# Single matmuls with their own waits in the first projection groups, and the last tile's stores and square sums block by block, in a hybrid encoder layer

## The chip, the cores and the metric

The kernel runs on the 8 cores of one Trainium2 chip, one stream of the prompt batch and two of the 16 decode streams on each core, with no exchange between cores. The metric is the device time of the slowest core in microseconds (us).

## The reference, cut to what matters

One layer of a streaming encoder (D_MODEL 1024, 8 prompt streams of 8192 frames, 16 sample streams of 16 frames, FFN width 2816):

```python
h = rms_norm(x, p['norm_mix_g'])
u, q, k, v, gl = jnp.split(h @ p['w_in'], SPLITS, axis=-1)
u, new_rnn_conv = causal_dwconv(u, ...)            # width 4
y_rnn, new_h = rglru(u, ...)                       # gates, recurrence
q = rms_norm(q ...); k = rms_norm(k ...)           # per head
y_attn, ... = banded / cached window attention     # ALiBi, sinks
g_rnn, g_attn = jnp.split(jax.nn.sigmoid(gl + p['b_gate']), 2, axis=-1)
mixed = g_rnn * (y_rnn @ p['w_rnn_proj']) + g_attn * (y_attn @ p['w_attn_proj'])
x = x + mixed @ p['w_out']
h2 = rms_norm(x, p['norm_ffn_g'])
a, b = jnp.split(h2 @ p['w_up'], 2, axis=-1)
a, new_ffn_conv = causal_dwconv(a, ...)            # width 3
x = x + (jax.nn.gelu(a) * b) @ p['w_down']
# rms_norm: x * rsqrt(mean(x * x) + 1e-6) * g
```

Outputs are x of both kinds of streams and their new states.

## The kernel before

Activations lie with the 128 features of a block on the partitions and the frames in the free dimension. The prompt stream of a core is cut into NT = 16 tiles of 512 frames; a tile of x is 8 blocks of 128 x 512 in `xt`, which has two buffers. The sample streams (32 columns) go along with tile 0 and share its weights.

A tile has a front half and a back half. The front half is the first norm (`n1`, which writes the 8 blocks of `hTa`), the K, Q, U and V projections with their norms, convolution and recurrence, and the attention (units "K", "Q", "U", "V", "A"). The back half is `mid` (gates and the two branch projections, which write `mq`), `outp` (output projection, residual add, and the second norm, which writes `hTb`), `up` and `down` (the FFN). Class "F" is the front of a tile, class "B" the back of the one before; the two run beside each other, except for the front of tile 0 and the back of tile 15.

A projection group is `mm8`: eight (or six) matmuls of 128x128 weights by 128x512 into one PSUM bank, added as one operation that waits for all its inputs ahead of its first matmul. Its weights are a block in `ring`, which has 11 slots. In tile 0 the blocks come as float32 through GpSimd's queue, which casts them (`ring<-wb`), and SyncE stores each one as bf16 to the scratch `wsc` once it has landed; later tiles load them from there on SyncE's queue (`ring<-wsc`). `load_x` sends four loads of 512 KB on SyncE's queue for each tile.

The order of the instructions is planned ahead. Each operation has a due value `P.v` (smaller is earlier), an engine, and a duration from a small model (`t_pe`, `t_act` and others). `schedule` simulates the engines and takes for each one the ready operation with the smallest due value (ring loads strictly in order); the result is a fixed list for each of the five queues, with semaphore waits between them. The matmul groups of a class share a key, "chainF" or "chainB", so they keep the order in which they were added. The due values of the front of tile 0 start at -1.0 + 0.36 for K0 and grow with the cost of the units (K 3, Q 3, U 7, V 1, A 4, in all 122 for a span of 0.61).

A norm sums the squares of the 8 blocks. `norm_begin(s, nsum)` says how many of them are summed ahead: ScalarE squares each block, GpSimd adds the first nsum squares into one buffer, and TensorE sums that and each of the other squares over the partitions by matmuls with a matrix of ones (L721). With nsum = 1, GpSimd adds nothing and TensorE does one ones matmul per block. The squares have three buffers (`sq`). Before, `outp` uses 6 in every tile, and `n1` uses 1 in tile 0 and 8 in the others. `norm_end` takes Ln and Exp (L728, L730) and scales the blocks on VectorE (L733).

`down` writes back x: block m's residual add (L1081) follows its three groups, and after blocks 3 and 7 one store of 1 MB goes to `yp` on SyncE's queue (L1085). The kernel ends when SyncE has seen all DMA semaphores at their last values.

Of the kernel before, what the change touches and what calls it, by code (L numbers as in the profile page):

```python
# [17 lines left out]
class _DSem:  # L18
    def __init__(self, sem, name):
        self.sem = sem  # L20
        self.name = name
        self.count = 0
        self.last = None
# [56 lines left out]
class Prog:  # L80
    def __init__(self, nc):
        self.nc = nc
        self.ops = []
        self.last_writer = {}
        self.readers = {}
        self.stack = contextlib.ExitStack()
        self.eng_sems = {}
        for e in ("pe", "act", "dve", "pool"):
            self.eng_sems[e] = self.stack.enter_context(nc.semaphore("s_" + e))
        self.dsems = []  # L90
        self.v = 0.0
        self.cls = "B"

    def sbuf(self, name, shape, dtype):
# [321 lines left out]
def t_dve(n):  # L416
    return 0.17 + n / 960.0
# [10 lines left out]
def t_pe(n):  # L428
    return max(n / 2370.0, 0.061)


def build_program(T):
    assert T % 512 == 0
    NT = T // 512
# [5 lines left out]
    def dout(name, shape, dt=F32):  # L440
        return nc.dram_tensor(name, list(shape), dt, kind="ExternalOutput").ap()
# [15 lines left out]
    yp = dout("yp", [NT, 128, 8, 512])  # L457
# [12 lines left out]
    P = Prog(nc)  # L470
    xt = P.sbuf("xt", [128, 2, 8, 512], F32)
# [67 lines left out]
    def sbf(pool, s):  # L539
        return Buf(SMALL[pool.name] if s.id == "s" else pool)  # L540


    d_x = [[P.dsem(f"x{b}{q}") for q in range(4)] for b in range(2)]
    d_y = [[P.dsem(f"y{b}{q}") for q in range(2)] for b in range(2)]
# [11 lines left out]
    def load_x(t):  # L556
        b = t % 2
        for q in range(4):
# [9 lines left out]
          writes=[("hu", s, n) for s in (1, 2) for n in range(8)])  # L568
    P.dma(lambda e: e.dma_start(out=st[:, ST_H + 8:ST_H + 24], in_=sst_d[:, 48:64]), d_c[2],
          writes=[("sh", s, n) for s in (1, 2) for n in range(8)])  # L570
    P.dma(lambda e: e.dma_start(out=st[:, ST_FH + 44:ST_FH + 132], in_=sst_d[:, 64:152]), d_c[3],
          writes=[("fh", s, n) for s in (1, 2) for n in range(NFB)])
# [12 lines left out]
          reads=BT1, writes=BT2, dur=1.3)  # L585
    P.add("dve", lambda e: e.tensor_tensor(out=btf, in0=btf, in1=btf2, op=ALU.max), reads=BT2, writes=BT1, dur=2.3)
    for h in range(8):
# [6 lines left out]
          reads=["prm"], writes=["dv_c"], tset="E")  # L594
    P.add("act", lambda e: e.activation(out=dv[:, DV_CH:DV_CH + 8], in_=dv[:, DV_CH:DV_CH + 8], func=AF.Ln, bias=1.0),
          reads=["dv_c"], writes=["dv_c"], tset="E")
# [11 lines left out]
          reads=["prm"], writes=["dv_esk"], tset="E")  # L608
# [12 lines left out]
    def weight(ti, blk, third=False):  # L621
        buf = Buf(RING)
        n = 768 if third else 1024
        src = w3_d if third else wb_d
        sc = wsc3 if third else wsc
        key = ("w3" if third else "w", blk)
        v0 = P.v
        P.v = v0 - 0.04
        when = 0 if (blk < 50 and not third) else (0, 0, 0, 1, 2)[blk % 5]
        if ti <= when:  # L630
            P.dma(lambda e: e.dma_start(out=buf.t[:, 0:n], in_=src[blk, :, :]), None, reads=XG, writes=[buf], queue="pool", nbytes=128 * n * 4,
                  ringload=True)
            if ti == when:
                ds = d_wst[wst_n[0] % 8]
                wst_n[0] += 1
                P.v = v0
                P.dma(lambda e: e.dma_start(out=sc[blk, :, :], in_=buf.t[:, 0:n]), ds, reads=[buf], writes=[key], nbytes=128 * n * 2)
        else:
            P.dma(lambda e: e.dma_start(out=buf.t[:, 0:n], in_=sc[blk, :, :]), None, reads=[key], writes=[buf], nbytes=128 * n * 2,
                  ringload=True)  # L640
        P.v = v0
        return buf

    def mm8(wbuf, rhs, rkeys, W, nk=8, pbuf=None, start=True, stop=True, k0=0, hold=()):
        if pbuf is None:
            pbuf = Buf(PS)
        fns = []
        for kc in range(nk):
            fns.append(lambda e, kc=kc: e.matmul(pbuf.t[:, 0:W], lhsT=wbuf.t[:, kc * 128:(kc + 1) * 128], rhs=rhs(k0 + kc),  # L649
                                                 start=start and kc == 0, stop=stop and kc == nk - 1))  # L650
        P.add("pe", fns, reads=[wbuf] + list(rkeys), writes=[pbuf, "chain" + P.cls] + list(hold), dur=nk * t_pe(W))
        return pbuf

# [44 lines left out]
    def norm_begin(s, nsum):  # L698
        s.nps = Buf(PS, "G")
        s.nsum = nsum  # L700
        s.nacc = sbf(LT, s)

    def norm_part(s, m):
        W = s.W
        nps, acc = s.nps, s.nacc
        last = s.nsum - 1
        if m == 0 and last > 0:
            P.add("act", lambda e: e.activation(out=acc.t[:, 0:W], in_=s.x(0), func=AF.Square), reads=[s.xk(0)], writes=[acc],
                  dur=t_act(W))
            return  # L710
        sqb = sbf(SQ, s)
        P.add("act", lambda e: e.activation(out=sqb.t[:, 0:W], in_=s.x(m), func=AF.Square), reads=[s.xk(m)], writes=[sqb],  # L712
              dur=t_act(W))
        if m < last:
            P.add("pool", lambda e: e.tensor_tensor(out=acc.t[:, 0:W], in0=acc.t[:, 0:W], in1=sqb.t[:, 0:W], op=ALU.add),  # L715
                  reads=[sqb, acc], writes=[acc], dur=t_pool(W))
            return
        if m == last and last > 0:
            P.add("pool", lambda e: e.tensor_tensor(out=sqb.t[:, 0:W], in0=acc.t[:, 0:W], in1=sqb.t[:, 0:W], op=ALU.add),
                  reads=[sqb, acc], writes=[sqb], dur=t_pool(W))  # L720
        P.add("pe", lambda e: e.matmul(nps.t[:, 0:W], lhsT=onesb[:, :], rhs=sqb.t[:, 0:W], start=(m == last), stop=(m == 7)),  # L721
              reads=[sqb, "onesb"], writes=[nps], dur=t_pe(W))

    def norm_end(s, pg, dst, dkeys):
        W = s.W
        nps = s.nps
        r = sbf(LT, s)
        P.add("act", lambda e: e.activation(out=r.t[:, 0:W], in_=nps.t[:, 0:W], func=AF.Ln, bias=EPS, scale=1.0 / D),  # L728
              reads=[nps], writes=[r], dur=t_act(W, 1), tset="E")
        P.add("act", lambda e: e.activation(out=r.t[:, 0:W], in_=r.t[:, 0:W], func=AF.Exp, scale=-0.5), reads=[r], writes=[r],  # L730
              dur=t_act(W), tset="E")
        for kc in range(8):
            P.add("dve", lambda e, kc=kc: e.scalar_tensor_tensor(out=dst(kc), in0=s.x(kc), scalar=prmc(pg + kc, 1),  # L733
                                                                 in1=r.t[:, 0:W], op0=ALU.mult, op1=ALU.mult),
                  reads=[s.xk(kc), r, "prm"], writes=[dkeys[kc]], dur=t_dve(W))
# [285 lines left out]

    def outp(t, ss, va, vbb):
        for s in ss:
            norm_begin(s, 6)
        for m in range(8):
            P.v = va + (vbb - va) * m / 8.0
            wb = weight(t, B_O + m)
            for s in ss:
                ps = mm8(wb, s.mq, [("mq" + s.id, k) for k in range(8)], s.W)
                P.add("dve", lambda e, s=s, ps=ps, m=m: e.tensor_tensor(out=s.x(m), in0=ps.t[:, 0:s.W], in1=s.x(m), op=ALU.add),  # L1030
                      reads=[ps, s.xk(m)], writes=[s.xk(m)], dur=t_dve(s.W))
                norm_part(s, m)
        P.v = vbb
        for s in ss:
            norm_end(s, P_GF, s.hb, [("hb" + s.id, kc) for kc in range(8)])
# [33 lines left out]
    def down(t, ss, va, vbb):  # L1069
        b = t % 2  # L1070
        for m in range(8):
            P.v = va + (vbb - va) * m / 8.0
            wbs = [weight(t, B_D0 + m), weight(t, B_D1 + m), weight(t, m, third=True)]
            for s in ss:
                W = s.W
                ak = "act" if s.id == "p" else "acts"
                ps = Buf(PS)
                for i, wb in enumerate(wbs):
                    nk = 8 if i < 2 else 6
                    mm8(wb, s.ac, [(ak, 8 * i + k) for k in range(nk)], W, nk=nk, pbuf=ps, start=(i == 0), stop=(i == 2), k0=8 * i)  # L1080
                P.add("dve", lambda e, s=s, ps=ps, m=m: e.tensor_tensor(out=s.x(m), in0=ps.t[:, 0:s.W], in1=s.x(m), op=ALU.add),  # L1081
                      reads=[ps, s.xk(m)], writes=[s.xk(m)], dur=t_dve(W))
            if m % 4 == 3:
                q = m // 4
                P.dma(lambda e, q=q: e.dma_start(out=yp[t, :, 4 * q:4 * q + 4, :], in_=xt[:, b, 4 * q:4 * q + 4, :]), d_y[b][q],  # L1085
                      reads=[("x", b, 4 * q + i) for i in range(4)], queue="sp", nbytes=1048576)
        for s in ss:
            if s.id == "s":
                P.dma(lambda e: e.dma_start(out=ys[:, :, :], in_=xss[:, :, :]), d_fin, reads=[("xs", m) for m in range(8)])
# [194 lines left out]
```

How the kernel before makes its waits and increments, by code:

```python
        def emit(name, e, tail=False):  # L354
            for op in streams.get(name, []):
                for sem, val in op.waits:
                    e.wait_ge(sem, val)
                ins = None
                for fn in op.fns:
                    ins = fn(e)
                if op.is_dma:
                    ins.then_inc(op.dsem.sem, 16)
                elif op.needs_sig:
                    ins.then_inc(eng_sems[name], 1)
            if tail:
                for sem, val in finals:
                    e.wait_ge(sem, val)
```

## Time and profile before

| | |
|---|---|
| median of 3 runs | 3942.33 us (4266.44, 3921.73 and 3942.33) |
| profiled execution | 3919.15 us, span of its slowest core 3917.5 us |
| spans of the eight cores | 3899.3 to 3917.5 us |
| TensorE (PE) busy | 3779.3 us, 96% of the span |
| VectorE (DVE), ScalarE (ACT), GpSimd (POOL) busy | 2591.8, 2808.4, 464.6 us |
| mean granted clock of TensorE, slowest core | 0.991 |

The profile is of one execution, on its slowest core, core 6. A line of it names the line of the kernel (L649), the engine, the operation, and the tiles it writes and reads (out<-in). "PE" is the matmul part of TensorE, "PEld" its weight loads, "SPq" the queue of SyncE. Idle time stands with what ended it.

### The profile page before, as it was taken

Reading aid. Unit: us, or ns where it says so; the run is one execution under the profiler, and the core shown is the slowest. Engines: PE = TensorE matmul, PEld = TensorE weight load, DVE = VectorE, ACT = ScalarE, POOL = GpSimd, SP = SyncE. Lnnn points to the kernel's source line nnn. Section 1 sums busy time; section 2 is a strip of 40 time slices with the busy share of each in tenths; the row PEclk is TensorE's granted clock in tenths of the full one; section 3 lists DMA queues with packets and bytes.
Section 4 is the critical chain, followed back from the end, with each engine's and each line's share of the span. In section 5 each row is a group of like instructions: output and inputs, shape, how many; then the busy total and the mean of one; then the engine's idle time right before and its main releaser. Section 6 shows DMA issues by size and latency. Waiting matters only on the chain.

```text
span 3917.5 us, 65207 instructions; the slowest of 8 cores (3899.3 to 3917.5 us)
## 1 busy us (share of the span) xinstructions
PE 3779.3 (96%) x18209; PEld 1746.1 (45%) x18576; DVE 2591.8 (66%) x4718; ACT 2808.4 (72%) x4636; POOL 464.6 (12%) x984
## 2 busy tenths in 40 slices
PE   5789999999999999999999999999999999999989
PEld 2344444444444444444444444444444444444434
DVE  6667476675757757576675757767576675757634
ACT  6778586776868768686776868768686776868641
POOL 2222111111010010101001010010111001011000
PEclk9899999999999999999999999999999999999999
DMA  9598767566464554646446464554645455464544
GB/s 187 117 191 175 199 157 195 149 159 193 134 186 138 157 163 138 190 135 183 141 144 182 134 186 138 160 163 139 188 138 181 140 148 175 139 186 140 159 133 140
DMA packets 325198, 626.69 MB, mean 160 GB/s; under 512 B 36784, under 2 KB 55376, under 8 KB 320720
## 3 DMA queue, kind: packets, MB, share of 16 engines
q1 hardware_dynamic: 299936, 577.87, 49.4%
q0 software_dynamic: 24912, 44.64, 8.1%
q8 instruction: 161, 2.64, 0.3%
q14 instruction: 189, 1.55, 0.1%
HBM read 600.36 MB, written 67.09 MB: 170 GB/s over the span
## 4 chain that ended last, share of the span: by engine, by line
PE 85%; DVE 5%; DMA 4%; ACT 3%; issue 3%; POOL 0%; SPq 0%; DVEq 0%; ACTq 0%; POOLq 0%
PE ps L649 78%; DVE hTb L733 2%; DMA xt<-xp 2%; PE ps L907 1%; PE ps L828 1%; PE ps L963 1%; PE ps L937 1%; DMA yp<-xt 1%; DMA ring<-wb 1%; PE ps L958 1%; DMA ring<-wsc 1%; PE ps L873 1%; DVE fset L754 0%; ACT L970 0%; PE ps L721 0%
## 5 line engine op out<-in xcount | busy, mean ns | idle before, releaser
L649 PE MATMUL ps<-hTb,ring 128*128 128x512 bf16 x5517 | 1259.8, 379 | 33.5 <-DVE hTb L733 18.2
L649 PE MATMUL ps<-hTa,ring 128*128 128x512 bf16 x4246 | 1003.3, 383 | 20.1 <-DMA ring<-wsc 5.8
L649 PEld LDWEIGHTS ps<-hTb,ring 128*128 128x128 bf16 x5632 | 547.0, 98 | 693.6 <-issue 45.3
L649 PEld LDWEIGHTS ps<-hTa,ring 128*128 128x128 bf16 x4352 | 426.1, 99 | 529.6 <-issue 37.2
L649 PE MATMUL ps<-actb,ring 128*128 128x512 bf16 x2762 | 629.0, 380 | 3.4 <-issue 0.2
L754 DVE SCALAR_TENSOR_TENSOR tt<-ps,prm_s,tt 128x511 f32<-128x511 f32 x704 | 522.0, 745 | 50.3 <-POOL tt L750 23.2
L649 PEld LDWEIGHTS ps<-actb,ring 128*128 128x128 bf16 x2816 | 275.8, 98 | 332.5 <-issue 3.2
L747 ACT ACTIVATE tt<-ps,prm_s 128x512 f32<-128x512 f32 x352 | 271.1, 771 | 133.0 <-PE ps L649 131.4
L996 ACT ACTIVATE tt<-ps,dv 128x512 f32<-128x512 f32 x256 | 173.8, 679 | 265.2 <-PE ps L649 256.7
L1065 DVE TENSOR_TENSOR actb<-ps,tt 128x512 bf16<-128x512 f32 x352 | 238.6, 684 | 145.2 <-PE ps L649 144.7
L754 DVE SCALAR_TENSOR_TENSOR fset<-ps,prm_s,fset 128x511 f32<-128x511 f32 x372 | 276.6, 744 | 21.5 <-POOL fset L750 11.6
L1008 DVE TENSOR_TENSOR mq<-ps,tt 128x512 bf16<-128x512 f32 x128 | 88.4, 691 | 274.0 <-PE ps L649 118.1
L830 ACT ACTIVATE fset<-ps,dv 128x512 f32<-128x512 f32 x248 | 157.0, 684 | 150.6 <-PE ps L828 150.1
L715 POOL TENSOR_TENSOR lt<-lt,sq 128x512 f32<-128x512 f32 x154 | 180.0, 1169 | 624.3 <-ACT sq L712 617.4
L649 PE MATMUL ps<-yr,ring 128*128 128x512 bf16 x1003 | 233.9, 380 | 1.3
L649 PE MATMUL ps<-ya,ring 128*128 128x512 bf16 x1003 | 232.9, 379 | 1.1
L649 PE MATMUL ps<-mq,ring 128*128 128x512 bf16 x1003 | 225.1, 379 | 3.2 <-DVE mq L1018 1.6
L1081 DVE TENSOR_TENSOR xt<-ps,xt 128x512 f32<-128x512 f32 x128 | 87.9, 687 | 211.6 <-PE ps L649 211.5
L1061 ACT ACTIVATE tt<-tt 128x512 f32<-128x512 f32 x352 | 205.6, 622 | 18.3 <-DVE tt L754 13.3
L750 POOL TENSOR_TENSOR tt<-tt,hcf 128x2 f32<-128x2 f32 x330 | 76.2, 231 | 1186.9 <-ACT tt L747 1186.5
L1015 DVE TENSOR_TENSOR mb<-ps,tt 128x512 bf16<-128x512 f32 x128 | 88.3, 690 | 176.8 <-ACT tt L1000 92.4
L943 ACT ACTIVATE pT<-lt 128x512 bf16<-128x512 f32 x254 | 155.9, 623 | 41.8 <-DVE lt L940 38.3
(193 smaller groups left out, 4781.6 us busy)
## 6 DMA issues: line engine op xcount, KB each, us to landing
ring<-wsc SPq DMA_DIRECT2D x1731, 256.0 KB, 2.7
ring<-wb POOLq DMA_DIRECT2D x157, 256.0 KB, 6.1
xt<-xp SPq DMA_DIRECT2D x64, 512.0 KB, 6.8
yp<-xt SPq DMA_DIRECT2D x32, 1024.0 KB, 5.3
wsc<-ring SPq DMA_DIRECT2D x118, 256.0 KB, 5.5
ring<-wsc SPq DMA_DIRECT2D x117, 192.0 KB, 2.4
ring<-w POOLq DMA_DIRECT2D x11, 192.0 KB, 5.7
wsc<-ring SPq DMA_DIRECT2D x8, 192.0 KB, 5.7
```

The source lines that it names most:

```text
L649: fns.append(lambda e, kc=kc: e.matmul(pbuf.t[:, 0:W], lhsT=wbuf.t[:, kc * 128:(kc + 1) * 128], rhs=rhs(k0 + kc), start=start and kc == 0, ...
L715: P.add("pool", lambda e: e.tensor_tensor(out=acc.t[:, 0:W], in0=acc.t[:, 0:W], in1=sqb.t[:, 0:W], op=ALU.add), reads=[sqb, acc], writes=[ ...
L747: P.add("act", lambda e: e.activation(out=acc()[:, 0:W], in_=ps.t[:, 0:W], func=AF.Identity, bias=bcol, scale=wcol(ntap - 1)), reads=[ps] ...
L754: P.add("dve", lambda e, k=k: e.scalar_tensor_tensor(out=segv(acc()[:, 0:W], s)[:, :, k:L], in0=segv(ps.t[:, 0:W], s)[:, :, 0:L - k], scal ...
L830: P.add("act", lambda e, pg=pg, col=col, dvc=dvc: e.activation(out=fs.t[0][:, col, 0:W], in_=pg.t[:, 0:W], func=AF.Exp, scale=-1.0, bias=d ...
L943: P.add("act", lambda e, sb=sb, pt=pt, nk=nk: e.activation(out=pt.t[0:nk, 0:N], in_=sb.t[0:nk, 0:N], func=AF.Exp), reads=[sb], writes=[pt] ...
L996: P.add("act", lambda e, g=g, ps=ps, half=half, m=m, W=W: e.activation(out=g.t[:, 0:W], in_=ps.t[:, 0:W], func=AF.Exp, bias=dv[:, DV_NBG + ...
L1008: P.add("dve", lambda e, g=g, ps=ps, s=s, m=m, W=W: e.tensor_tensor(out=s.mq(m), in0=ps.t[:, 0:W], in1=g.t[:, 0:W], op=ALU.mult), reads=[g ...
L1015: P.add("dve", lambda e, g=g, ps=ps, mb=mb, W=W: e.tensor_tensor(out=mb.t[:, 0:W], in0=ps.t[:, 0:W], in1=g.t[:, 0:W], op=ALU.mult), reads= ...
L1061: P.add("act", lambda e, g=g, W=W: e.activation(out=g.t[:, 0:W], in_=g.t[:, 0:W], func=AF.Gelu), reads=[g], writes=[g], dur=t_act(W), tset ...
L1065: P.add("dve", lambda e, g=g, ps=ps, s=s, i=i, W=W: e.tensor_tensor(out=s.ac(i), in0=ps.t[:, 0:W], in1=g.t[:, 0:W], op=ALU.mult), reads=[g ...
L1081: P.add("dve", lambda e, s=s, ps=ps, m=m: e.tensor_tensor(out=s.x(m), in0=ps.t[:, 0:s.W], in1=s.x(m), op=ALU.add), reads=[ps, s.xk(m)], wr ...
```

## The change

A new value `vsplit` = -0.61 stands in the program. In `mm8`, where a group has a key for each of its inputs and its due value is below `vsplit`, each of its matmuls is added as an operation of its own, which waits for its own input block only. In the last tile, `norm_begin` in `outp` is called with 1 in place of 6, and `down` stores each block of x on its own (256 KB), on the eight semaphores of the x loads.

```diff
+        self.vsplit = -0.61
...
         for kc in range(nk):
             fns.append(lambda e, kc=kc: e.matmul(pbuf.t[:, 0:W], lhsT=wbuf.t[:, kc * 128:(kc + 1) * 128], rhs=rhs(k0 + kc),
                                                  start=start and kc == 0, stop=stop and kc == nk - 1))
+        if len(rkeys) == nk and P.v < P.vsplit:
+            for kc in range(nk):
+                P.add("pe", fns[kc], reads=[wbuf, rkeys[kc]], writes=[pbuf, "chain" + P.cls] + (list(hold) if kc == 0 else []), dur=t_pe(W))
+            return pbuf
         P.add("pe", fns, reads=[wbuf] + list(rkeys), writes=[pbuf, "chain" + P.cls] + list(hold), dur=nk * t_pe(W))
         return pbuf
...
     def outp(t, ss, va, vbb):
         for s in ss:
-            norm_begin(s, 6)
+            norm_begin(s, 6 if t < NT - 1 else 1)
...
-            if m % 4 == 3:
-                q = m // 4
-                P.dma(lambda e, q=q: e.dma_start(out=yp[t, :, 4 * q:4 * q + 4, :], in_=xt[:, b, 4 * q:4 * q + 4, :]), d_y[b][q],
-                      reads=[("x", b, 4 * q + i) for i in range(4)], queue="sp", nbytes=1048576)
+            st_ = 4 if t < NT - 1 else 1
+            if m % st_ == st_ - 1:
+                m0 = m + 1 - st_
+                P.dma(lambda e, m0=m0: e.dma_start(out=yp[t, :, m0:m0 + st_, :], in_=xt[:, b, m0:m0 + st_, :]),
+                      d_y[b][m0 // 4] if t < NT - 1 else d_x[m % 2][m // 2],
+                      reads=[("x", b, m0 + i) for i in range(st_)], queue="sp", nbytes=262144 * st_)
```

## Rows read from the trace of the kernel before

**Rows 1.** The page: its head, busy time, and the span in 40 slices.
```profile
span 3917.5 us, 65207 instructions; the slowest of 8 cores (3899.3 to 3917.5 us)
...
PE 3779.3 (96%) x18209; PEld 1746.1 (45%) x18576; DVE 2591.8 (66%) x4718; ACT 2808.4 (72%) x4636; POOL 464.6 (12%) x984
...
PE   5789999999999999999999999999999999999989
```

**Rows 2.** Timeline, VectorE and TensorE, 16 to 30 us.
```profile
16.25 5.39 DVE L733 SCALAR_TENSOR_TENSOR hTa<-xt,prm_s,lt 128x512 bf16<-128x512 f32 x8 [1.83 <-ACT lt L730]
...
21.55 1.38 DVE L733 SCALAR_TENSOR_TENSOR hTas<-xss,prm_s,lt_s 128x32 bf16<-128x32 f32 x8
...
21.89 3.57 PE L649 MATMUL ps<-hTa,ring 128*128 128x512 bf16 x8 [4.64 <-DVE hTas L733]
...
25.51 2.99 PE L649 MATMUL ps<-hTa,ring 128*128 128x512 bf16 x8
...
29.55 1.89 PE L649 MATMUL ps<-hTa,ring 128*128 128x512 bf16 x8 [0.62 <-ACT sq L871]
```

**Rows 3.** Timeline and waits of SyncE's queue, and GpSimd's issues, to 30 us.
```profile
18.37 0.33 SPq L637 DMA_DIRECT2D wsc<-ring  x1
...
28.73 0.32 SPq L637 DMA_DIRECT2D wsc<-ring  x1
...
SPq L357 <- DMA ring<-wb: 22.3, 4, 10.0
...
22.90 2.13 POOL L631 DMA_DIRECT2D ring<-wb  x4
...
26.28 0.54 POOL L631 DMA_DIRECT2D ring<-wb  x1 [1.24 <-PE ps L649]
```

**Rows 4.** Windows: busy PE, PEld, DVE, ACT, POOL; granted clock, DMA share, GB/s.
```profile
20.00:30.00 10.00, 7.49 (x37) 3.23 (x39) 2.94 (x11) 2.09 (x6) 6.28 (x13) 1.00 1.06 186
60.00:160.00 100.00, 62.43 (x319) 25.76 (x323) 75.62 (x212) 74.55 (x200) 12.44 (x22) 0.78 0.51 113
80.00:120.00 40.00, 26.38 (x112) 10.07 (x113) 29.67 (x83) 27.40 (x76) 2.65 (x5) 0.67 0.43 103
```

**Rows 5.** Chain of work, 20 to 66 us: start, us, what.
```profile
26.28 24.85 DMA ring<-wb
...
51.62 12.81 DMA xt<-xp
```

**Rows 6.** Timeline of ScalarE, 25 to 66 us.
```profile
25.55 0.60 ACT L871 ACTIVATE sq<-ps 128x512 bf16<-128x512 f32 x1 [7.70 <-PE ps L649]
...
64.79 0.63 ACT L708 ACTIVATE lt<-xt 128x512 f32<-128x512 f32 x1 [4.43 <-DMA xt<-xp]
```

**Rows 7.** Timeline, output projection and norm of tile 15.
```profile
3771.76 13.97 PE L649 MATMUL ps<-mq,ring 128*128 128x512 bf16 x63 [1.58 <-DVE mq L1018]
...
3784.34 1.16 POOL L719 TENSOR_TENSOR sq<-lt,sq 128x512 bf16<-128x512 f32 x1 [0.85 <-ACT sq L712]
...
3785.84 0.69 DVE L1030 TENSOR_TENSOR xt<-ps,xt 128x512 f32<-128x512 f32 x1 [1.03 <-PE ps L649]
3786.68 0.63 ACT L712 ACTIVATE sq<-xt 128x512 bf16<-128x512 f32 x1 [1.09 <-DVE xt L1030]
...
3794.99 2.72 PE L649 MATMUL ps<-hTb,ring 128*128 128x512 bf16 x6 [7.16 <-DVE hTb L733]
```

**Rows 8.** Timeline of the end, from 3894 us.
```profile
3894.13 0.32 SPq L639 DMA_DIRECT2D ring<-wsc  x1
...
...
3912.19 0.34 SPq L1085 DMA_DIRECT2D yp<-xt  x1
```

**Rows 9.** DMA, 3906 to 3918 (40 slices); last, ring loads, 3860 to 3918.
```profile
DMA  0000000000000000000000099999989400000000
...
yp<-xt SPq DMA_DIRECT2D x1, 1024.0 KB, 4.1
...
DMA to landing us min/median/max: 2.3/2.7/4.3
```

## Prediction

> **What bounds the kernel now.** I read the page first: TensorE is busy for 3779.3 of 3917.5 us [rows 1], so only 138 us of the span are not matmul, and a change that removes no large group of matmuls can move the end only by what it does to those gaps. The slices of the page show where they are: the digits of PE are below 9 in the first three slices (294 us) and in the last but one [rows 1]. So two places matter, the start of tile 0 and the end of tile 15, and the change touches just these. Between them every slice reads 9.
>
> At the start, the timeline shows that the first projection group (K0, eight matmuls) begins at 21.89 us, 4.64 us after TensorE's last work, and that what it waited for is VectorE: the eight hTa blocks take 5.39 us from 16.25 on [rows 2]. It looks like a plain 5 us to be had. But the queue of SyncE tells of the weights. Each ring slot, once its weight block has landed, is stored to the scratch by SyncE, in order; of these stores K1's goes out at 18.37, K0's before it, and U0's not before 28.73, after a wait for ring<-wb of 10.0 us [rows 3]. So U0's weights land at about 28.7, and its group starts at 29.55 [rows 2]: the third group has 0.85 us of room and no more. The DMA share of the stretch is 1.06 [rows 4], so the loads don't come sooner for being awaited sooner. Further on the chain of work runs over DMA altogether: the load issued at 26.28 lands 24.85 us later, the load of the next tile's x goes out behind it at 51.62 and takes 12.81 us [rows 5], and ScalarE, whose order is fixed, sits idle for 4.43 us until 64.79 for that very x [rows 6]. From there to about 160 us, tile 0 alone, with nothing of another tile's back half beside it, is bound by short chains of TensorE, ScalarE and VectorE: TensorE is busy for 62.43 us of 100 at a granted clock of 0.78 [rows 4].
>
> At the end, the output projection of tile 15 runs without a gap (63 recorded matmuls in 13.97 us), then comes the norm: residual add, square, ones matmul, Ln, Exp, eight hTb blocks of the same kind and shape as hTa's, and the next group 7.16 us after TensorE's last work [rows 7]. After the last matmul there are a residual add (0.69 us for one of this shape [rows 7]), a store of 1 MB issued at 3912.19 [rows 8], and its landing 4.1 us after its issue [rows 9].
>
> **The change, part by part.**
>
> *Which groups are split.* The due value of K0 is -0.64, of K1 -0.625, of U0 -0.61, and -0.61 is not below -0.61 (in floating point neither). So four groups, K0 and K1 for the prompt and for the 32-column sample stream, become 32 single operations. The back halves start at 0. Nothing is added to TensorE's work.
>
> *Start of tile 0.* K0's last matmul can't start before the eighth hTa block is done at 21.64; with the 0.25 us that lie between that and the 21.89 of before [rows 2], it ends at about 22.3. The chain key keeps the order K0, K0 sample, K1. The sample blocks hTas are done at 21.55 + 1.38 = 22.93, so K1 starts at about 23.2 in place of 25.51 [rows 2]: 2.3 us earlier. Its eight matmuls cost 0.427 us each (3.57 for eight, the lower of the two clock levels, 1.2 GHz) to 0.216, so K1 ends 1.9 to 3.4 us sooner. Then U0 is next, and its weights come at 28.7: at most 29.55 - 28.73 = 0.8 us of this gets past it. The norm steps of K0 and K1 on ScalarE (idle for 7.70 us ahead of the square at 25.55 [rows 6]) move into idle time. On the other path, the ring load at 26.28 waited for K0's slot; GpSimd, busy with issues to 25.03 [rows 3], can send it the 1.24 us of its wait earlier, into queues that are full (1.06), so the landing at 51.1 and the x after it gain between 0 and 1.24 us. I take -0.4 us, near the lower end, because both full queues [rows 4, 5] and the late U0 weights speak against more. The bounds are 0 and -3.4.
>
> *Waits in a row.* The split puts up to eight waits on TensorE's queue where one stood. Behind them stand only the same groups, which could not have run earlier; V0 and V1, whose weights were there, stay behind U0. A wait costs no more than the 0.25 us above, and only the last of each group lies on the path: already counted.
>
> *Squares of tile 15 on TensorE.* Removed: five GpSimd adds (four at 1.16 us each and the one at 3784.34, which ends at 3785.5) and with them the wait for them. None is on the path: the add of block 5 is over at 3785.50, before the residual add of block 7 starts at 3785.84, and the chain goes on from that one over its square at 3786.68 [rows 7]. Added: five ones matmuls, for blocks 0 to 4. Before, three ran, for 5 and 6 after the last projection matmul, in the shade of block 7's add, and for 7. A square is ready some 1.8 us after its group ends (0.05 + 0.69 + 0.10 + 0.63 and the signals), a group lasts 1.73, so by the list's rule (lowest due value among what is ready) the matmuls for 0 to 4, and the one for 5 too, once the groups have grown longer by them, come ahead of the last projection group. That is six of 0.216 us (16 matmuls in 3.62 less the pipeline's end; 0.216 by the spacing) = 1.3 us on a stretch where TensorE has no gap; five would be 1.1. Squares hold one of three buffers until a matmul has read it, instead of an add: no new wait, at one square per 1.9 us. So +1.3 us, bounds 0 and +1.5. The 7.16 us wait for hTb is as before, since nothing of tile 15 is split, and with it the matmuls at the lower clock behind it (six in 2.72 us [rows 7]).
>
> *Stores per block.* Eight of 256 KB in place of two of 1 MB, on their own semaphores, last used by loads long landed. Six more issues of 0.34 us on SyncE's queue, each of which waits for its residual add, with ring loads behind. The last ring load goes out at 3894.13 for a group that starts after 3906 [rows 8], so the loads run eleven slots ahead; a store holds the queue for a block's add and its own issue, 0.69 + 0.34, about 1 us against over 12: hidden, at nothing. If that cover were gone it would cost up to eight times 1 us. The last store now carries a quarter. In the row of the last store the DMA engines are at work in some eight and a half slices of 0.3 us, 2.5 us for 1.05 MB [rows 9]; a quarter of that is 0.6, so 1.9 us less. By the nearest rows of that size, ring loads of 192 to 256 KB at 2.3 to 4.3 us from issue to landing, median 2.7 [rows 9], it would be 1.8 to -0.2, with a median of 1.4. I take -1.7, between the two and nearer to the first, which is of this very store; bounds -1.9 and 0.2.
>
> The Trainium skill (DMA: Bandwidth & Descriptors, section Bandwidth) speaks against small transfers: batch to 1 MiB or more for three quarters of peak. Its fit for a GpSimd-issued transfer (section Anatomy of one DMA) is a fixed 2.0 us plus size over 436 GB/s; taken over to this store as an estimate, that gives 4.4 and 2.6 us, so 1.8 us less where the sum has 1.7. The row's 4.1 us is near the 4.4. The rule is about throughput, and here only the last landing is on the path.
>
> **Sum.** -0.4 + 1.3 - 1.7 = -0.8 us on a profiled execution of 3919.15 us: 3918.3. The two timed runs that are of use for it lie 2.6 and 23.2 us above the profiled one (3921.73 and 3942.33; the third is 8% off and says nothing of the kernel). I set the lower of the two shifts on top: **3921 us**, no change. The median of 3942.33 is that of the shown three and is itself one of those two runs.
>
> **The rivals.**
>
> *The whole start is passed on.* If the U0 weights are not what holds U0 (nearer loads can land sooner on other cores), the 3.0 us and more of K1's end go straight through. For it: from 66 to 160 us nothing but latency bounds, so a shift would stay. Against it: rows 3 and the 4.43 us wait for x. Price -3.4 in place of -0.4: 3918 us.
>
> *The upper clock comes earlier.* Before, TensorE stood idle for 4.64 us ahead of K0 and ran K0 at 0.427 us a matmul. After, it has a matmul every 0.67 us from 16.9 on, and K1 may run wholly at 0.216 (2.4 GHz). K1 then ends 3.4 us sooner and not 1.9, and if those 1.5 us reach the end beside what the sum has, it is 3919.5 us. U0's late weights are against it. The Trainium skill (TensorE: Matmul & The Clock Gate, section The HAM clock gate) says that the idle state is the throttled one and that activity lifts it, which is that mechanism.
>
> *Slower: the list is planned anew.* The order of all engines comes from a list planner with its own durations. In its plan K0 and K1 end 2 to 3 us earlier, so from 22 us on close calls on five queues fall otherwise, and this may cost more than the edits bring. The place is ScalarE's wait for the next tile's x [rows 6]: the squares stand in its queue at a planned place. If they come two or three operations earlier, x lands no sooner, and ScalarE's idle 4.43 us grow by as much work, up to double; and from there on nothing hides it until 160 us. With more gaps, the clock falls as in the stretch of 80 to 120 us (granted 0.67, TensorE busy for 26.38 of 40 us [rows 4]); 20 us more of such a stretch, with 13.2 us of matmul at 0.67 in place of the 0.78 of the whole, give 2.2. Together 4.4 + 2.2 = 6.6: 3928 us. It decides once the squares are planned before the work that now fills ScalarE up to 60.36. For it: the eight cores, with one program, already differ by 18.2 us in span (3899.3 to 3917.5 [rows 1]). Against it: it can as well go the other way.
>
> *It doesn't do what it says.* If SyncE's or VectorE's blocks come too late for the split, only the end is changed: -0.4: 3921 us, not to be told apart.
>
> **How the numbers follow.** No change as summed 0.55; whole start passed on 0.13 and earlier clock 0.07, both to be read as up to 3 us faster; planned anew and slower 0.20; without effect 0.05. No case comes near 2% (78 us), about what a measurement of this kernel can tell from no change. So the range is set less by the cases (3918 to 3928, and 3915 to 3930 with the bounds of the terms) than by how the runs scatter: 18 us between cores, 20.6 between the two runs. I take 3904 to 3944. Faster by over 2%: 0.01; slower: 0.01, for a planner gone astray; within: 0.98.
>
> **What would show it.** Right: the first K0 matmul near 17 us and K1 ending by 25 to 27, with U0 still at 28.7 to 29.5; x of tile 1 landing at 64 to 65. The ones matmuls between the groups of the last output projection, and hTb's first block 1.3 us further behind the projection's first matmul than the 17.6 us of now. The last store landing 2.3 to 2.7 us after issue. Wrong: U0 starting with K1's end, or TensorE's busy time and clock in 60 to 160 us off by over 4 us; a store in the last tile with a ring load behind it that a group waits for.

## The result, and the profile after

The changed kernel takes 3950.99 us (median of 18 runs, 3941.66 to 4677.77) against 3937.27 us of the kernel before beside it (18 runs, 3921.73 to 4539.34). The ratio is 1.0046, 95% interval 1.0026 to 1.0066: about 18 us slower (0.46% of 3.94 ms), small beside 2% but clear of no change, and above the range of the prediction. A few executions of both kernels are disturbed by some per cent; the ratios leave these out.

The page of the changed kernel, head, busy time, slices:

```profile
span 3957.5 us, 65593 instructions; the slowest of 8 cores (3922.1 to 3957.5 us)
...
PE 3817.1 (96%) x18581; PEld 1750.7 (44%) x18581; DVE 2589.5 (65%) x4718; ACT 2803.5 (71%) x4634; POOL 457.6 (12%) x979
...
PE   5788999999999999999999999999999999999989
```

Against [rows 1] the eight spans have moved as a whole: mean 3935.6 us in place of 3911.3, so 24.3 us. That is one execution of each, and the profiled one of before (3919.15 us) was quicker than all of the 18 timed ones, so the 24.3 us say more than the ratio's 18. (The busy sum of TensorE can't be compared: the trace of before lacks some matmul records, x18209 beside x18581.) One digit has changed, the fourth slice, 9 to 8: about 297 to 396 us. The page after is that of core 3, though, and the page before that of core 6; on core 6 no digit has changed. The start and the end, which the prediction read, show in the timeline of TensorE on core 6 what was expected of them, or more:

```profile
17.05 0.59 PE L650 MATMUL ps<-hTa,ring 128*128 128x512 bf16 x1 [0.37 <-DVE hTa L738]
17.43 0.23 PE L726 MATMUL ps<-sq_s,onesb 128*128 128x32 bf16 x1
17.61 4.56 PE L650 MATMUL ps<-hTa,ring 128*128 128x512 bf16 x7
...
23.48 2.72 PE L650 MATMUL ps<-hTa,ring 128*128 128x512 bf16 x6
...
26.07 1.01 PE L650 MATMUL ps<-hTa,ring 128*128 128x512 bf16 x2
...
28.09 1.67 PE L650 MATMUL ps<-hTa,ring 128*128 128x512 bf16 x7 [0.80 <-ACT sq_s L876]
```

K0's first matmul is at 17.05 in place of 21.89, K1 begins at 23.48 in place of 25.51, U0 at 28.09 in place of 29.55 [rows 2]. At the other end, the norm of tile 15 and the DMA slices of 3906 to 3926 us on core 6:

```profile
3780.39 5.34 PE L650 MATMUL ps<-mq,ring 128*128 128x512 bf16 x24 [1.58 <-DVE mq L1023]
...
3804.86 1.44 PE L650 MATMUL ps<-hTb,ring 128*128 128x512 bf16 x3 [7.16 <-DVE hTb L738]
```
```profile
DMA  6400049000000009400000004900000000940000
...
yp<-xt SPq DMA_DIRECT2D x4, 256.0 KB, 2.0
```

Projection to hTb takes 24.47 us in place of 23.23 [rows 7], and the last store lands 2.0 us after its issue in place of 4.1 [rows 9]. These two nearly cancel. So the loss is in neither place that the diff touches.

To find it I compared the starts of the same groups, core by core, in the two timelines. Tile 0's first output-projection group (`ps<-mq,ring`) starts at 219.8 us before (mean of eight cores, 214 to 222) and at 235.8 after (232 to 239). Tile 1's starts at 486.9 before and 511.5 after, tile 3's at 960.0 and 984.0. So 16 us are lost by the start of tile 0's output projection, 8.6 more by tile 1's, and nothing after that. (By how much such starts scatter among kernels with the same list is said with the table below.) TensorE on core 6 at the first of these places, before and then after:

```profile
217.79 1.89 PE L649 MATMUL ps<-ya,ring 128*128 128x512 bf16 x8
219.51 0.35 PE L649 MATMUL ps<-yas,ring 128*128 128x32 bf16 x8
219.72 1.91 PE L907 MATMUL ps<-wvs,hTa 128*128 128x256 bf16 x16
222.29 1.67 PE L649 MATMUL ps<-mq,ring 128*128 128x512 bf16 x7 [0.67 <-DVE mb_s L1015]
...
240.46 1.89 PE L649 MATMUL ps<-hTa,ring 128*128 128x512 bf16 x8
```
```profile
217.74 1.89 PE L650 MATMUL ps<-ya,ring 128*128 128x512 bf16 x8
219.47 0.35 PE L650 MATMUL ps<-yas,ring 128*128 128x32 bf16 x8
221.96 0.83 PE L650 MATMUL ps<-hTa,ring 128*128 128x512 bf16 x2 [2.14 <-DMA ring<-wsc]
...
225.14 2.13 PE L912 MATMUL ps<-wvs,hTa 128*128 128x256 bf16 x16
231.94 3.14 PE L650 MATMUL ps<-hTa,ring 128*128 128x512 bf16 x8 [4.66 <-DMA ring<-wsc]
234.87 2.36 PE L650 MATMUL ps<-mq,ring 128*128 128x512 bf16 x8
```

The last `ya` groups of tile 0 start within 0.05 us of each other in the two kernels: the 1.5 us won at U0 are gone by then. After is even one group behind, because U2 of tile 1 ran ahead of this `ya` group before and runs behind it after, at 221.96, where its weights are late by 2.14 us. Then the order differs once more. Before, the output projection runs at once, and the K0 group of tile 1 (`hTa`) comes behind it, at 240.46. After, this K0 group stands ahead of the output projection. Its weights are not there: TensorE waits 4.66 us, with the eight `mq` groups behind it. The chain of work there (start, us, what):

```profile
196.64 11.07 DMA ring<-wb
...
207.84 11.03 DMA wsc<-ring
...
218.94 12.76 DMA ring<-wsc
...
231.94 5.30 PE ps L650 x16
```

The 256 KB block for K0 is a load from the scratch on SyncE's queue. Three transfers hang on each other here by the ring slot that they share: a casting load of GpSimd fills the slot (11.07 us), SyncE stores the block to the scratch (11.03 us), and only when this store has landed, and TensorE has used the block, may the load for K0 overwrite the slot. It goes out at 218.94 and lands 12.76 us later. The queue ahead of it is held up too: its stores wait for casting loads to land (SyncE's waits from 205 to 240 us: 21.8 us in 9 waits for `ring<-wb`). The load isn't later than before, where K0's load goes out at 222.76, behind six stores; it is the group that now wants it at 227 us and not at 240. TensorE's waits for `ring<-wsc` from 100 to 520 us on core 6, before, then after:

```profile
PE ps L649 <- DMA ring<-wsc: 5.8, 3, 2.9
```
```profile
PE ps L650 <- DMA ring<-wsc: 15.0, 6, 4.7
```

(us in total, times, longest.) Over the eight cores these sums are 2.5 to 5.8 us before and 15.0 to 24.2 after. The idle time is not all of the loss. With the output projection late, what follows from it is late, and less is there to run: from 205 to 245 us TensorE is busy for 32.80 us in place of 37.36, at a clock of 0.91 in place of 1.00 (same columns as [rows 4]):

```profile
205.00:245.00 40.00, 37.36 (x293) 20.01 (x298) 23.72 (x54) 28.18 (x66) 16.26 (x25) 1.00 0.97 201
```
```profile
205.00:245.00 40.00, 32.80 (x228) 16.94 (x231) 20.64 (x47) 22.89 (x55) 7.13 (x14) 0.91 0.87 180
```

### The profile page after: what moved, and what is told of

It reads as the page before. It is cut to its first block, busy times and chain, and to the rows that moved or that the text cites. A ratio compares the mean times of both kernels' runs of the same rounds, so it can differ in the third digit from the quotient of the medians.

```text
span 3957.5 us, 65593 instructions; the slowest of 8 cores (3922.1 to 3957.5 us)
## 1 busy us (share of the span) xinstructions
PE 3817.1 (96%) x18581; PEld 1750.7 (44%) x18581; DVE 2589.5 (65%) x4718; ACT 2803.5 (71%) x4634; POOL 457.6 (12%) x979
## 4 chain that ended last, share of the span: by engine, by line
PE 83%; DMA 7%; DVE 4%; ACT 2%; issue 2%; POOL 1%; SPq 0%; DVEq 0%; ACTq 0%; POOLq 0%
PE ps L650 77%; DMA xt<-xp 2%; DVE hTb L738 2%; DMA yp<-xt 2%; DMA ring<-wsc 1%; DMA ring<-wb 1%; PE ps L912 1%; PE ps L968 1%; PE ps L833 1%; PE ps L942 1%; PE ps L963 1%; PE ps L878 1%; ACT L975 0%; DVE fset L759 0%; POOL lt L720 0%
## 5 line engine op out<-in xcount | busy, mean ns | idle before, releaser
L650 PE MATMUL ps<-hTb,ring 128*128 128x512 bf16 x5632 | 1272.6, 380 | 23.3 <-DVE hTb L738 18.2
L650 PE MATMUL ps<-hTa,ring 128*128 128x512 bf16 x4352 | 1018.6, 384 | 26.5 <-DMA ring<-wsc 24.2
L650 PEld LDWEIGHTS ps<-actb,ring 128*128 128x128 bf16 x2816 | 275.7, 98 | 332.5 <-issue 3.4
```

## The experiments

The theory after the result: the list was planned anew, because in the planner's simulation K0 and K1 end earlier, and a close call then fell the wrong way, tile 1's K0 group ahead of tile 0's output projection. The main rival: the added waits themselves cost time. In the table "mq0" and "mq1" are the starts of the first output-projection group of tile 0 and tile 1, "span" the mean of the eight spans, each in us and a mean over the cores in the profiled execution. "All" is the mean of the eight spans over all executions that enter the ratio, with their number. Lines of helpers shift by a few from kernel to kernel; the tiles' names say which group is meant.

| kernel | ratio [95%] | mq0 | mq1 | span | all |
|---|---|---|---|---|---|
| before | | 219.8 | 486.9 | 3911.3 | 3912.7 to 3913.7 (12, 23, 18) |
| after | 1.0046 [1.0026, 1.0066] | 235.8 | 511.5 | 3935.6 | 3937.2 (13) |
| split only | 1.0052 [1.0037, 1.0068] | 233.0 | 503.5 | 3932.6 | 3929.4 (6) |
| end only | 0.9997 [0.9975, 1.0019] | 219.2 | 489.8 | 3912.6 | 3913.1 (10) |
| waits only | 1.0006 [0.9993, 1.0018] | 220.2 | 485.9 | 3906.4 | 3912.8 (10) |
| plan only | 1.0062 [1.0046, 1.0077] | 233.6 | 509.2 | 3935.9 | 3931.2 (4) |
| K0 held | 1.0010 [0.9978, 1.0042] | 222.4 | 489.9 | 3913.7 | 3916.9 (8) |
| K0 first | 1.0018 [0.9988, 1.0048] | 231.8 | 503.1 | 3925.1 | 3923.1 (4) |
| loads swapped | 1.0041 [1.0013, 1.0068] | 231.3 | 500.2 | 3923.1 | 3928.3 (12) |
| K0 split | 1.0045 [1.0018, 1.0072] | 231.5 | 506.0 | 3932.0 | 3927.8 (9) |
| best | 0.9977 [0.9949, 1.0005] | 220.3 | 491.2 | 3911.6 | 3908.6 (6) |
| plan late | 1.0005 [0.9985, 1.0025] | 228.0 | 499.5 | 3919.0 | 3916.1 (10) |
| plan slow | 1.0007 [0.9990, 1.0024] | 219.4 | 503.3 | 3921.5 | 3923.0 (8) |

Before ran beside the other kernels in three sets, so it has three values in the last column. Beside after, its spans weren't kept; by its slowest core it was some 8 us longer there than in the later sets, so 3937.2 can't be set against them. A standard error of 0.5 to 2 us belongs to each value of the last column (from the scatter of the executions).

End only, waits only and best have the list of before up to tile 14, split only and plan only that of after: the planner does not see the waits or the last tile's edits there. So the scatter of one profiled execution can be read off. With before's list mq0 is 219.2 to 220.3 and mq1 comes 265.7 to 270.9 us later; with after's list mq0 is 233.0 to 235.8 and mq1 270.5 to 275.7 us later. By the means of the two groups the new list costs 14.3 us at mq0 and 5.3 us more at mq1.

**Split only.** The split of the groups, with the last tile as before.

```diff
-            norm_begin(s, 6 if t < NT - 1 else 1)
+            norm_begin(s, 6)
...
-            st_ = 4 if t < NT - 1 else 1
+            st_ = 4
...
-                      d_y[b][m0 // 4] if t < NT - 1 else d_x[m % 2][m // 2],
+                      d_y[b][m0 // 4],
```

> Only the split of the four K groups; the end of the last tile is as before. The theory (the split changes the planned order on all queues, and in tile 0 and 1 loads of tile 1's weights then stand behind stores that wait for cast loads): the whole loss is here, 3946 to 3956 us, ratio 1.003 to 1.007, TensorE idle for weights between 215 and 235 us. The rival that the edits at the end cost it: the time of before, ratio 0.998 to 1.001.

Measured 1.0052, the whole of the loss; by the last column 15.7 us, less than the 24.3 us between the two profiled executions.

**End only.** No group is split; ones matmuls and stores of tile 15 as in the change.

```diff
-        self.vsplit = -0.61
+        self.vsplit = -9.99
```

> Only the edits at the end of the last tile (ones matmuls for all squares, eight stores); no split. By the sum: +1.3 us in the output projection and -1.7 us at the last landing, so the time of before within 2 us (ratio 0.999 to 1.001), and both terms to be read in the trace. The rival that the end costs the time: ratio 1.003 to 1.007.

Measured 0.9997 [0.9975, 1.0019]: the edit of the last tile neither costs nor brings anything that can be told.

**Waits only.** The group stays one planned operation, so each queue keeps the order of before; only at emission does each matmul wait for its own block.

```diff
+        op = P.add("pe", fns, reads=[wbuf] + list(rkeys), writes=[pbuf, "chain" + P.cls] + list(hold), dur=nk * t_pe(W))
+        if len(rkeys) == nk and P.v < P.vsplit:
+            op.late = {P.last_writer[rkeys[kc]]: kc for kc in range(nk)}
...
-                for fn in op.fns:
+                for i_, fn in enumerate(op.fns):
+                    for sem, val in wt.get(i_, ()):
+                        e.wait_ge(sem, val)
                     ins = fn(e)
```

> The planned order of before on every queue, but each matmul of K0 and K1 (both streams) waits for its own block only; the end as before. If the wait itself costs or brings something it is seen here: by the sum -0.4 us, so ratio 0.998 to 1.001, with K0's first matmul near 17 us and U0's group still at 28.7 to 29.5. The theory of the planned order says the same: no loss. A rival in which the waits block TensorE says 1.003 or more.

**Plan only.** The reverse: single operations in the planner, so its order is that of split only, but after planning the first matmul of a group waits for all blocks (`lw` holds their writers).

```diff
+                o_ = P.add("pe", fns[kc], reads=[wbuf, rkeys[kc]], writes=[pbuf, "chain" + P.cls] + (list(hold) if kc == 0 else []), dur=t_pe(W))
+                if kc == 0:
+                    o_.grp = lw
...
         for op in order:
+            if op.grp:
+                op.deps = set(op.deps) | set(op.grp)
```

> The planned order of split_only on every queue, but the first matmul of each K group waits for all eight blocks, as before the change; the end as before. The theory of the planned order: the whole loss stays, ratio 1.003 to 1.007, TensorE idle between 215 and 235 us. The rival of the waits: the time of before.

These two decide the main question. Waits only: K0 starts at 16.59 and U0 at 27.25, two us ahead of before, as early as in the changed kernel, and the ratio is 1.0006 [0.9993, 1.0018]. Plan only: K0 starts at 20.90, so the early start is taken away, and the ratio is 1.0062 [1.0046, 1.0077], with the output projection behind the K0 group of tile 1 again (core 6):

```profile
220.50 1.91 PE L921 MATMUL ps<-wvs,hTa 128*128 128x256 bf16 x16
229.92 3.57 PE L656 MATMUL ps<-hTa,ring 128*128 128x512 bf16 x8 [7.51 <-DMA ring<-wsc]
233.28 2.65 PE L656 MATMUL ps<-mq,ring 128*128 128x512 bf16 x8
```

The waits cost nothing; the order of the list carries the loss.

**K0 held.** The split, and one rule for the planner: tile 1's K0 group (`k0[0]`) only after the seventh output-projection block of tile 0 (`mq[6]`).

```diff
     def finish(self, pen=0.1, bw=300000.0):
+        k0[0].deps.add(mq[6][0].idx)
         self.schedule(pen, bw)
```

> The plan of split_only, with one more rule for the planner: the K0 group of tile 1 comes after the first matmul group of block 6 of tile 0's output projection, as it stands in the order of before. The theory (K0 of tile 1, whose weights come late, stands in front of output projection groups that are ready): the first output projection group starts at 220 to 226 us again in place of 231 to 236, and the ratio falls from 1.0052 to 1.000 to 1.003. The rival that the loss comes from the order of tile 0's front or of SyncE's queue in itself: 1.004 to 1.007, as split_only.

**K0 first.** No split at all, and the opposite rule.

```diff
+        mq[0][0].deps.add(k0[0].idx)
         self.schedule(pen, bw)
```

> The order of before (no split, end as before), with one rule put into the planner: the first output projection group of tile 0 comes after the K0 group of tile 1. The theory: this alone brings the loss, first output projection group at 230 to 236 us, ratio 1.002 to 1.006. The rival (the position of this group is of no matter): 0.998 to 1.001.

Core 6 with K0 held, then with K0 first:

```profile
220.16 1.91 PE L917 MATMUL ps<-wvs,hTa 128*128 128x256 bf16 x16
222.29 1.89 PE L655 MATMUL ps<-mq,ring 128*128 128x512 bf16 x8 [0.23 <-DVE mq L1028]
```
```profile
219.95 1.91 PE L917 MATMUL ps<-wvs,hTa 128*128 128x256 bf16 x16
230.72 3.26 PE L655 MATMUL ps<-hTa,ring 128*128 128x512 bf16 x8 [8.87 <-DMA ring<-wsc]
233.81 1.89 PE L655 MATMUL ps<-mq,ring 128*128 128x512 bf16 x8
```

Held, the output projection starts where it did before, the waits for `ring<-wsc` on core 6 are 2.2 us, and the mean span is within 2.4 us of before's. Put first in a kernel that is otherwise before's, the group brings a wait of 8.87 us, 12 of the 16 us at mq0 and 13.8 of the 24.3 us of the mean span. The timed ratios, which go by the slowest core, say less: 1.0010 and 1.0018, with intervals that touch both 1 and the changed kernel's; by them alone, K0 held could still be 0.4% slower, and K0 first no slower at all. The last column tells them apart: K0 first is 10.4 us longer than before (3923.1 against 3912.7), K0 held 4.2 us, where split only is 15.7. K0 held keeps U2 of tile 1 behind the last `ya` group, as after has it, which may be its 2.6 us at mq0.

**Loads swapped.** The split; on SyncE's queue each load from the scratch of tile 1 that stands right behind a 256 KB store goes one place ahead of it.

```diff
+        for o in [o for o in sp if o.ringload and o.v < 0.5]:
+            i = sp.index(o)
+            if not sp[i - 1].ringload and sp[i - 1].nbytes == 262144:
+                sp[i - 1], sp[i] = sp[i], sp[i - 1]
```

> split_only, with every load of tile 1's weights on SyncE's queue, where it stands right behind a store to the scratch and is due before 0.5, put one place ahead of that store (six to seven such swaps); nothing else of the order is changed. If the loads are late because they stand behind stores that wait for cast loads, each is issued 2 to 5 us sooner and TensorE's waits for ring from the scratch fall from 14 to 20 us to 6 to 14: ratio 1.001 to 1.004. If they are late by the full DMA queues only: as split_only, 1.004 to 1.007.

Measured 1.0041 [1.0013, 1.0068], mq0 231.3, 1.7 us sooner than in split only; the last column has 3928.3 in place of 3929.4. TensorE's waits for `ring<-wsc` are 8.2 to 17.3 us, on six cores within the 6 to 14 expected. The chain of core 6 shows why one place on the queue brings so little:

```profile
192.06 10.24 DMA ring<-wb
...
202.42 12.51 DMA wsc<-ring
...
215.00 8.99 DMA ring<-wsc
```

The moved load goes out at the moment at which the store of the block that stood in its ring slot has landed; so it does on seven of the eight cores, where these stores take 10.97 to 14.01 us. What holds the load is its slot as much as its place on the queue.

**K0 split.** Only K0 of tile 0 is split (bound -0.63). The planner gives here too an order with K0 of tile 1 ahead of the output projection (K1 of tile 1 comes right behind the first group of it, not ahead as the expectation has it), so this is a test on a kernel that the theory was not made from.

```diff
-        self.vsplit = -0.61
+        self.vsplit = -0.63
```

> Only the groups of K0 are split (threshold -0.63 in place of -0.61), the end as before. The planned order that this gives has not only K0 of tile 1 but K1 of tile 1 too ahead of the output projection. The theory: a smaller edit at the start, and the loss is there all the same, first output projection group at 234 to 242 us, ratio 1.003 to 1.008. The rival that the loss grows with the number of split groups: half of that of split_only, 1.002 to 1.003.

Measured 1.0045 [1.0018, 1.0072], mq0 231.5, below the 234 to 242 us expected. Half of the split costs as much as the whole: what counts is the order that comes out. The mean of mq0 is mixed, though: on cores 4 and 5 TensorE is busy without a gap from 180 to 220 us at a granted clock of 0.81 in place of 1.00, core 5 has no wait for weights there at all, and core 4's 238.0 is of the clock. The six other cores give 230.5.

**Best.** The order of before with the waits by block as in waits only, also in the first hTb group of tile 15, and that tile's stores per block; its squares stay on GpSimd.

```diff
+        if len(rkeys) == nk and (P.v < P.vsplit or P.v == P.vlast):
+            op.late = {P.last_writer[rkeys[kc]]: kc for kc in range(nk)}
...
+            st_ = 4 if t < NT - 1 else 1
```

> The planned order of before; the four K groups and the first group on the last tile's hTb wait block by block where they stand; the last tile's stores by block; the square sums as before (GpSimd, six). By the terms: -0.4 for the start, -3 for hTb (its eight matmuls paced by VectorE's 0.67 us in place of 3.4 us behind it), -1.7 for the last store: -5 us, ratio 0.9975 to 1.000.

TensorE of core 6, the first hTb blocks:

```profile
3791.64 0.38 PE L659 MATMUL ps<-hTb,ring 128*128 128x512 bf16 x1 [2.42 <-DVE hTb L745]
3792.30 0.38 PE L659 MATMUL ps<-hTb,ring 128*128 128x512 bf16 x1 [0.29 <-DVE hTb L745]
```

The wait is 2.42 us in place of 7.16 [rows 7], and from the output projection's first matmul to the issue of the last store it is 138.2 us in place of 140.4. The ratio is 0.9977 [0.9949, 1.0005]: it leans to faster, and can't be told from no change.

**Plan late, plan slow.** On top of best, the planner is told that the transfers of this stretch take longer, in the hope that it then puts no group ahead of its weights: all casting loads and the scratch loads of tile 1 land 8 us later, or the bandwidth is three quarters up to tile 1.

```diff
-                op.end = dma_free + 1.9
+                op.end = dma_free + 1.9 + (8.0 if op.eng == "pool" or (op.ringload and op.v < 1.0) else 0.0)
```
```diff
-                dma_free = begin + op.nbytes / bw
+                dma_free = begin + op.nbytes / (bw if op.v > 1.0 else 0.75 * bw)
```

> The kernel best, but the planner is told that cast loads, and loads of tile 1's weights, land 8 us later than it has believed. The order that this gives has the loads of tile 1 one to three stores further ahead on SyncE's queue and no K group ahead of the output projection. The theory (the loss comes from a plan that believes weights to be there too early): TensorE's waits for weights from the scratch fall below the 3 to 8 us of best, first output projection group at 216 to 222 us, ratio 0.994 to 0.999. The rival that any new plan is as good as another: anything from 0.998 to 1.006.

> The kernel best, but the planner reckons with three quarters of its DMA rate for all that is due before tile 1's back half, in place of a later landing. As plan_late by the theory: 0.994 to 0.999; by the rival 0.998 to 1.006. If the two differ, it tells whether it is the landing or the rate that the planner has wrong.

The waits for `ring<-wsc` did go: none from 100 to 520 us in the first, at most 1.5 us on a core in the second, where best has 3.4 to 8.0. The gain didn't come: 1.0005 and 1.0007, against 0.994 to 0.999 expected, and by the last column plan slow is 10 us longer than before, though its slowest core isn't. In plan late mq0 is 228.0 where 216 to 222 was expected; cores 2 and 3 have 239.8 and 240.3 there, at a granted clock of 0.81 from 180 to 220 us, and the six others 223.9 in the mean. mq1 is at 499.5 and 503.3, later than best's 491.2. In plan slow the time went into the stretch of 300 to 400 us; core 4, best, then plan slow (PE busy and count, clock, DMA share, GB/s):

```profile
300.00:400.00 100.00, 95.22 (x709) 1.00 0.92 174
```
```profile
300.00:400.00 100.00, 88.16 (x609) 0.97 0.78 155
```

The new orders have new waits elsewhere. I didn't follow these to a single operation.

## Why the prediction was wrong

**What failed.** The prediction gave "no change as summed" 0.55 and "planned anew and slower" 0.20. The second is what happened, for the reason that it names (the list's close calls fall otherwise, because K0 and K1 end earlier in its plan). So the sum failed by the term that it doesn't have: it leaves the new plan at nothing, where the runs show some 16 us. It was left out because the rival was priced at the wrong place, and this is the failed step: "The place is ScalarE's wait for the next tile's x". That wait did grow, from 4.43 us until 64.79 [rows 6] to this on core 6:

```profile
63.87 0.63 ACT L713 ACTIVATE lt<-xt 128x512 f32<-128x512 f32 x1 [6.92 <-DMA xt<-xp]
```

But x landed 0.9 us sooner, TensorE's busy time from 60 to 160 us is 60.73 us in place of 62.43 [rows 4], within the bound of 4 us that the prediction set, and at 217.8 us the two kernels are level. The place is 150 us further on, where tile 0's back half and tile 1's front first meet, and the engine is TensorE: its order is fixed too, and a group with late weights holds eight groups that are ready. The size followed from the place: 6.6 us were priced; some 18 were timed, and 15.7 by the last column of the table for the split alone.

**Why it could have been seen.** The reading stopped at 160 us, since every slice from the fourth on says 9. The window of 205 to 245 us of before, shown above, was there to be read: DMA share 0.97, and SyncE waits in it, in total, times, longest:

```profile
SPq L357 <- DMA ring<-wb: 27.6, 10, 6.9
```
A load from the scratch issued there stands behind stores that stand behind casting loads. TensorE had at that place two classes of ready work to choose from, of which one hung on this queue. The prediction's ground against the rival, "it can as well go the other way", is true of a plan with correct durations. The planner's are too short here: in its own simulation the three transfers of the chain above (casting load, store, load for K0) take 6.6, 6.9 and 6.3 us, against 11.07, 11.03 and 12.76 measured. That such a plan leans to one side, to put groups ahead of their weights, is argued and not shown: plan late and plan slow, with longer durations, lost the waits and not the time.

**Why the range failed.** It took 3904 to 3944 from the scatter of cores and runs, and its cases went up to 3928. At the size that the runs then showed (16 us at mq0, 24 in the profiled spans), the rival would have stood at 3937 to 3945 on the same base. Of the 30 us by which the forecast missed (3951 against 3921) some 18 are the change, by the ratio. The other 12 are the base: 3921 was the lower of two runs, and beside the change only 1 of the 18 executions of before came as low as 3922.

**Terms that held.** *Start:* K0 "near 17 us" was 17.05, K1 "at about 23.2" was 23.48, and it ended at 27.1 as foreseen at the later side. U0 came 1.5 us sooner (2.3 in waits only) where 0.8 was the most allowed. Its weights still held it, but they were not as fixed as taken: SyncE's store of U0's block, which waits for the same weights, goes out at 28.73 before, 27.81 after and 26.77 in waits only, and the group starts 0.8, 0.3 and 0.5 us behind it. It makes no odds: in waits only, which has the early start and the order of before, mq0 is at 220.2 against 219.8, so nothing of it is left, and "whole start passed on" is refuted. *Clock:* K1's matmuls are still spaced by 0.43 us until about 27, so the earlier activity didn't lift the clock in time for them, and that rival falls as well. The level is read from this spacing against 0.216 us; the granted clock of 20 to 30 us reads 1.00 in both kernels [rows 4] and doesn't tell the levels apart there. *Waits in a row:* at nothing, and waits only gives 1.0006. *Ones matmuls:* +1.3, measured 24.47 - 23.23 = +1.24. *Last store:* -1.7; from its issue to the end of the span 3.5 us in place of 5.3 [rows 8], so -1.8. The stores in between held up no load that a group waited for. The sum of the end, -0.4 forecast, is -0.6, and end only gives 0.9997.

**What stays open.** The cause of the first 16 us is shown: the order alone brings 14 of them (plan only), the rule takes all but 3 away (K0 held), the opposite rule brings 12 (K0 first). What the other group with late weights (U2, 2.14 us at 221.96) adds was not run by itself. The 8.6 us between mq0 and mq1, some 5 of them by the two groups of kernels and the rest scatter, look to be of the same kind by the waits: for `ring<-wsc` from 240 to 520 us TensorE waits 3.8 to 5.6 us in a core's mean with before's list and 8.2 to 10.9 with after's. No run isolates them. Also open is what the remaining misplacings in plan late and plan slow are, and whether any order is better than before's: of the seven others tried none was.

## What to carry to other kernels

In a kernel whose order comes from a planner, a local edit is two edits: what it does where it stands, and every close call that it moves downstream. Make it first with the order frozen (here: waits at emission, not new operations), and so separate the two. When reading the profile for such a change, look for the place where two classes of work meet on an in-order queue whose transfers land late, however far it lies behind the edit and whatever the slices say.

## What the runs showed of the hardware

A load of 256 KB from the scratch took 12.76 us from issue to landing at a DMA share of 0.87 to 0.97, with casting loads of GpSimd under way, where loads of 192 to 256 KB at the end of the kernel take 2.3 to 4.3 us [rows 9]. A lone store of 256 KB lands 2.0 us after issue, with about 0.65 us of full DMA share in the slices (a 9 and a 4 of 0.5 us each); 1 MB takes 4.1. TensorE with one 0.43 us matmul every 0.67 us from 17 us on is, by the spacing of its matmuls, still at the lower level (1.2 GHz) at about 27 us. And in best the granted clock falls to 0.50 soon after the shortened wait of tile 15, at 3793 us, and stays there to about 3799.5; the eight matmuls behind those that VectorE paces run 0.43 us apart, so part of what a shorter wait gives is taken back by the clock. In K0 split two cores of eight show a granted clock of 0.81 with TensorE busy without a gap, its matmuls 0.26 us apart in place of 0.216, while their neighbours are at 1.00.
